# A layer of hybrid mixers and a mixture of experts on one core: the last expert block's second weight and its turned rows in places of their own, overflow branches nested, filler transposes

## What is computed

```python
def s5_mixer(...):            # one of the three mixers
    ...
    z = jax.nn.gelu(y)
    out = z * jax.nn.sigmoid(z @ w_glu)          # "GLU", 1024x256 @ 256x256

def hier_moe(h, w_grp, b_grp, w_exp, b_exp, w1, w3, w2):
    g_sel = argmax(xf @ w_grp + b_grp)           # 1 of 4 groups
    top_p, top_i = top_k(softmax(exp_logits[rows, g_sel]), 2)   # 2 of its 8 experts
    ...
    def expert_block(xb, e):                     # a block: 128 rows of one expert
        hb = silu(xb @ w1[e]) * (xb @ w3[e])     # 1024 -> 512
        return hb @ w2[e]                        # 512 -> 1024
    return segment_sum(y_rows * gate, row_tok)

x = x + concat(mixers) @ w_out
x = x + hier_moe(rms_norm(x), ...)
```

## Time and profile before

| | |
|---|---|
| profiled execution, its own time | 1237.19 us |
| its span (first to last instruction) | 1235.0 us |
| PE busy | 1127.7 us (91%) |
| DVE busy | 972.1 us (79%) |
| ACT busy | 703.3 us (57%) |
| POOL busy | 388.1 us (31%) |
| moved from and to HBM | 252.25 MB read, 26.35 MB written |
| median of 3 runs | 1235.97 us |

### The profile page before, as it was taken

The page is one execution under the profiler, slowest core; times in us unless marked ns, Lnnn a source line. Parts: engine busy times, 40 slices in busy tenths (PEclk is TensorE's granted clock), DMA queues, the critical chain, the costliest instruction groups (busy, mean ns, idle before and its releaser), DMA issues.

```text
span 1235.0 us, 15931 instructions
## 1 busy us (share of the span) xinstructions
PE 1127.7 (91%) x5636; PEld 867.3 (70%) x5636; DVE 972.1 (79%) x1182; ACT 703.3 (57%) x820; POOL 388.1 (31%) x359
## 2 busy tenths in 40 slices
PE   5979999889999799994999999999999999999992
PEld 3437565656676577873788888888877877787781
DVE  1999999656766653377799999999989989898971
ACT  5611224655565541223577777777777777777751
POOL 2330007377971000113022232233343332233221
PEclk8989999899999899995899999999999999999996
DMA  6700010000005012227799999999999999999940
GB/s 196 177 1 1 0 19 10 2 1 1 2 1 239 1 35 85 102 103 279 312 378 369 369 392 385 386 394 396 382 361 380 373 358 371 373 349 367 356 136 10
DMA packets 55484, 260.93 MB, mean 211 GB/s; under 512 B 31088, under 2 KB 31760, under 8 KB 41616
## 3 DMA queue, kind: packets, MB, share of 16 engines
q1 hardware_dynamic: 45344, 243.03, 51.2%
q0 software_dynamic: 10096, 17.34, 5.9%
HBM read 252.25 MB, written 26.35 MB: 226 GB/s over the span
## 4 chain that ended last, share of the span: by engine, by line
PE 65%; DMA 13%; DVE 11%; ACT 4%; issue 4%; SPq 2%; POOL 1%; DVEq 0%; ACTq 0%; POOLq 0%
PE psum L2122 24%; DMA w<-in_w 12%; PE psum L2142 9%; PE psum L2034 7%; PE psum L1952 4%; PE psum L1762 3%; DVE arena L1112 3%; PE psum L1982 3%; PE psum L1800 3%; PE psum L1970 2%; PE psum L2112 2%; PE psum L1840 1%; DVE arena L1115 1%; DVE am L1439 1%; PE psum L1844 1%
## 5 line engine op out<-in xcount | busy, mean ns | idle before, releaser
L1606 DVE TENSOR_TENSOR w_rest<-w,w_high 128x2048 fp32r<-128x2048 f32 x136 | 305.2, 2286 | 19.0 <-ACT w_high L1033 18.5
L1033 ACT ACTIVATE w_high<-w 128x2048 fp32r<-128x2048 f32 x136 | 256.4, 1912 | 76.0 <-DMA w<-in_w 58.2
L2122 PE MATMUL psum<-w_high,xgT_high 128*128 128x512 f32 x544 | 217.7, 400 | 13.8 <-DVE xgT_rest L1652 13.8
L2122 PE MATMUL psum<-w_rest,xgT_high 128*128 128x512 f32 x544 | 213.7, 393 | 0.0
L2122 PE MATMUL psum<-w_high,xgT_rest 128*128 128x512 f32 x544 | 213.1, 392 | 0.0
L1659 DVE TENSOR_TENSOR w_rest<-w,w_high 128x2048 fp32r<-128x2048 f32 x68 | 152.5, 2284 | 2.1 <-ACT w_high L1043 2.1
L1043 ACT ACTIVATE w_high<-w 128x2048 fp32r<-128x2048 f32 x68 | 126.4, 1908 | 24.1 <-DMA w<-in_w 24.1
L2122 PEld LDWEIGHTS psum<-w_high,xgT_high 128*128 128x128 f32 x544 | 102.9, 189 | 39.2 <-issue 16.4
L692 POOL DMA_INDIRECT out<-arena,idx x34 | 94.5, 2780 | 107.3 <-DVE arena L1672 102.0
L2122 PEld LDWEIGHTS psum<-w_rest,xgT_high 128*128 128x128 f32 x544 | 102.8, 189 | 22.1
L2122 PEld LDWEIGHTS psum<-w_high,xgT_rest 128*128 128x128 f32 x544 | 103.1, 190 | 20.3
(11 more groups left out here) (272 smaller groups left out, 2029.8 us busy)
## 6 DMA issues: line engine op xcount, KB each, us to landing
w<-in_w SPq DMA_DIRECT2D x102, 2048.0 KB, 19.0
arena<-in_x SPq DMA_DIRECT2D x5, 1024.0 KB, 4.9
h_scratch<-arena SPq DMA_DIRECT2D x8, 512.0 KB, 2.6
out<-arena SPq DMA_DIRECT2D x8, 512.0 KB, 3.6
arena<-in_x SPq DMA_DIRECT2D x1, 3072.0 KB, 20.3
arena<-in_w_in SPq DMA_DIRECT2D x1, 2688.0 KB, 16.5
arena<-in_w_in SPq DMA_DIRECT2D x1, 2048.0 KB, 12.2
wout_y_raw<-in_w_out SPq DMA_DIRECT2D x1, 2048.0 KB, 9.1
```

What stands on the lines that cost most here:

```text
L1033: act.activation(w13h[k][:, c, :], w13[b][k][:, c, :], ACT.Copy).then_inc(W13H_READY[k], 1)
L1606: dve.tensor_tensor(w13l[b][k][:, c, :], w13[b][k][:, c, :], w13h[k][:, c, :].bitcast(F32), S_).then_inc(W13_SPLIT[k], 1)
L2122: last = pe.matmul(psum[:, k, :], x_[:, c, :], w_[:, c, :], start=(c == 0 and n == 0), stop=(c == KC - 1 and n == 2))
```

## The change

1. **Last block's second weight.** The high part of the last block's `w2` goes into `w1`'s high buffer (`w2h_last`), its turned hidden rows into the buffers of `xgT` (`heTh_last`, `heTl_last`), and its output into PSUM banks 0 and 1. ACT makes the two halves of `w2h_last` right after `high_heT(NS - 2)`, DVE takes the rests around `hidden(NS - 1)`, PE turns the last hidden rows between the two halves of `down(0, NS - 2)`.
2. **Overflow loop.** On all engines the second branch of a pass is nested in the first. On POOL the wait for the last scatter stands behind the loop (and inside it where a block is taken).
3. **Routing.** `picks_ready` and `slots_ready` are raised twice per part, so PE starts each product earlier; `table` runs k outermost.
4. **First gather.** POOL issues it straight from the table, then prepares the indices; DVE waits for `idxs_copied` before it goes on with `rest_w13` of block 0.
5. **Order at blocks 0 and 1.** PE does `turn_rows(1)` before `overflow_table()`, DVE `rest_xgT(1)` before it waits for that table.
6. **Filler transposes.** `keep_busy` writes transposes of `ident` to banks that nobody reads: 16 between the halves of `z`, 28, 28 and 36 in the routing, 14 after `turn_rows(0)`.

```diff
+        w2h_last = w13h[0].rearrange("p c n -> p (c n)").rearrange("p (f d) -> p f d", f=FC)
+        heTh_last, heTl_last = xgTh[:, 0:FC, :], xgTl[:, 0:FC, :]
...
# POOL
-            gather(0, 0)
+            settle()
+            pool.indirect_dma_start(out=xg[0], out_offset=None, in_=h2_d,
+                                    in_offset=bass.IndirectOffsetOnAxis(ap=tabi[:, 0, 0:1], axis=0),
+                                    bounds_check=T - 1, oob_is_err=False).then_inc(ROWS_IN[0], 16)
+            prepare(0, 0)
+            pool.tensor_copy(idx[:, 0, :], tabi[:, 0, :]).then_inc(idxg_copied, 1)
             gather(1, 1)
-            prepare(0, 0)
...
+            with pool.Fori(0, OVF // 2 - 1) as it:
+                with pool.If(n_ov > 2 * it + FIRST_OV):
+                    pool.wait_ge(Y_OUT[1], 8 * NS)
+                    ov_rows(0, it)
+                    with pool.If(n_ov > 2 * it + (FIRST_OV + 1)):
+                        ov_rows(1, it)
             pool.wait_ge(Y_OUT[1], 8 * NS)
-            with pool.Fori(0, OVF // 2 - 1) as it:
-                for b in range(2):
-                    with pool.If(n_ov > 2 * it + (FIRST_OV + b)):
...
# ACT
             high_heT(NS - 2)
+            act.wait_ge(W2_IN[1], 8 * NS)
+            for c in (slice(0, FC // 2), slice(FC // 2, FC)):
+                act.activation(w2h_last[:, c, :], w2s[1][:, c, :], ACT.Copy).then_inc(w2h_ready, 1)
+            act.wait_ge(heT_filled, NS)
+            act.activation(heTh_last.rearrange("p c n -> p (c n)"), psum[:, 2, :], ACT.Copy).then_inc(heTh_saved, 1)
             save_y(0, NS - 2)
-            for h in range(2):
-                high_w2(1, NS - 1, h, W2_IN[1], 8 * NS)
-            high_heT(NS - 1)
-            save_y(1, NS - 1)
...
# DVE
                 tt(both[:, i0:i1], pick[0][:, i0:i1], pick[1][:, i0:i1], A_)
+                dve.sem_inc(picks_ready, 1)
...
-                dve.sem_inc(slots_ready, 1)
+                for k in range(2):
+                    tt(rowhot[:, k, i0:i1, :], iota_j[:, :].unsqueeze(1).to_broadcast([P, n_t, P]),
+                       rw[:, k].unsqueeze(2).to_broadcast([P, n_t, P]), ALU.is_equal)
+                    dve.sem_inc(slots_ready, 1)
...
             dve.sem_inc(y_saved_v, 1)
+            dve.wait_ge(idxs_copied, 1)
             rest_w13(0, 0, 0, (1,))
...
# PE
+            def keep_busy(bank, n):
+
+                for _ in range(n):
+                    pe.transpose(bank[:, 0:P], ident[:, :], ident[:, :])
...
+                if c == 0:
+                    keep_busy(lo(F_Z(1, 1)), 16)
...
             table(0)
+            keep_busy(psum[:, 0, :], 28)
             ranks(1)
+            keep_busy(psum[:, 0, :], 28)
             table(1)
+            keep_busy(psum[:, 0, :], 36)
...
             turn_rows(0, 0, 16)
+            keep_busy(psum[:, 0, :], 14)
...
             up(1, 0, 0)
+            turn_rows(1, 1, 16)
             overflow_table()
-            turn_rows(1, 1, 16)
...
-            down(0, NS - 2)
-            turn_hidden(NS - 1)
-            down(1, NS - 1)
+            down(0, NS - 2, turn_last=True)
+
+            pe.wait_ge(heT_saved, NS)
+            pe.wait_ge(w2_split, 2 * NS)
+            parts = ((heTh_last, w2h_last), (heTl_last, w2h_last), (heTh_last, w2l[1]))
...
```

More of the change, by code:

```diff
@@ L1707, in _ @@
             hidden(0)
+            rest_xgT(1)
             dve.wait_ge(ov_filled, 1)
@@ L1710, in _ @@
             dve.sem_inc(ov_tab_ready, 1)
-            rest_xgT(1)
             rest_w13(1, 1, 1)
@@ L2075, in table @@
                 i0, i1 = ROUTE[part]
-                pe.wait_ge(slots_ready, part + 1)
-                for i in range(i0, i1):
-                    for k in range(2):
+                for k in range(2):
+                    pe.wait_ge(slots_ready, 2 * part + k + 1)
+                    for i in range(i0, i1):
                         last = pe.matmul(psum[:, 1, 0:2 * NE], rowhot[:, k, i, :], blkval[:, k, i].rearrange("p v e -> p (v e)"),
@@ L2129, in turn_hidden, with down @@
                 last.then_inc(heT_filled, 1)
-            def down(b, e):
+            def down(b, e, turn_last=False):
                 pe.wait_ge(heT_saved, e + 1)
@@ L2143, in down @@
                                              start=(c == 0 and n == 0), stop=(c == FC - 1 and n == 2))
+                    if turn_last and k == 0:
+                        turn_hidden(e + 1)
                 last.then_inc(y_filled, 1)
@@ L2169, in _, with ov_products @@
             up(1, 1, NS - 1)
-            down(0, NS - 2)
-            turn_hidden(NS - 1)
-            down(1, NS - 1)
+            down(0, NS - 2, turn_last=True)
+            pe.wait_ge(heT_saved, NS)
+            pe.wait_ge(w2_split, 2 * NS)
+            parts = ((heTh_last, w2h_last), (heTl_last, w2h_last), (heTh_last, w2l[1]))
+            for k in range(2):
+                for c in range(FC):
+                    for n, (h_, w_) in enumerate(parts):
+                        last = pe.matmul(psum[:, k, :], h_[:, c, :], w_[:, c, 512 * k:512 * (k + 1)],
+                                         start=(c == 0 and n == 0), stop=(c == FC - 1 and n == 2))
+            last.then_inc(y_filled, 1)
+            def ov_products(b, it):
+                e = 2 * it + (NS + b)
+                turn_rows(b, e, 16 * it + 16 * (NS // 2 + 1))
+                pe.wait_ge(xgT_saved, e + 1)
+                up(0, b, e)
+                up(1, b, e)
+                turn_hidden(e)
+                down(b, e)
             pe.wait_ge(ov_table, 1)
@@ L2176, in _ @@
             with pe.Fori(0, OVF // 2 - 1) as it:
-                for b in range(2):
-                    with pe.If(n_ov > 2 * it + (FIRST_OV + b)):
-                        e = 2 * it + (NS + b)
-                        turn_rows(b, e, 16 * it + 16 * (NS // 2 + 1))
-                        pe.wait_ge(xgT_saved, e + 1)
-                        up(0, b, e)
-                        up(1, b, e)
-                        turn_hidden(e)
-                        down(b, e)
+                with pe.If(n_ov > 2 * it + FIRST_OV):
+                    ov_products(0, it)
+                    with pe.If(n_ov > 2 * it + (FIRST_OV + 1)):
+                        ov_products(1, it)
 _INS = ["x", "positions", "mix_norm", "w_in", "q_a_norm", "w_uq", "kv_a_norm", "w_ukv", "q_norm", "k_norm",
```

111 lines of the change are left out of this document (66 added, 45 removed).

## The result

The changed kernel takes 1216.66 us, the median of 4 runs (1215.32 to 1220.37), against 1235.91 us for the kernel before on the same chip: a ratio of 0.986 with a 95% interval from 0.9835 to 0.9884, so 17.3 us less (14.3 to 20.4). The two medians by themselves lie 19.2 us apart, which this interval takes in. The forecast was 1219.0 us, its range 1212.5 to 1225.5. The profiled execution took 1220.37 us, the longest of the first four, with a span of 1218.5.

A forecast was written before the change was run, and what follows sets the result against it. The prediction took saturated DMA weight loads to bound the expert loop, with stalls in the chain at the end. Gains of 7.7 + 4.7 + 3.0 + 1.4 = 16.8 us from 1235.97 gave 1219.2, stated as 1219.0, range 1212.5 to 1225.5.

The forecast's parts named there:

- last block: End of the program: the stall before the last `down` goes, so the last scatter is issued at 1212.0 instead of 1219.74, 7.7 us less.
- loop ahead of the wait: POOL's overflow loop runs while the last scatter lands, with the DRAIN keeping its 5.96 us: 4.7 us less.
- GLU fillers: GLU product: 16 transposes in PE's 2.2 us gap keep the clock high, 6.8 instead of 9.88 us, 3.0 us less.
- routing to block 0: From ranks to block 0: first rank product and table leave the path, DVE becomes the bound, 1.4 us less.
- order at blocks 0 and 1: PE some 6 to 8 us ahead at block 1, but loads come no sooner: nothing gained at the end.
- rival 4: Stall before the last `down` partly stays because the last `w2` lands 3 us later than read: 1222 us; chance 0.07.
- the 0.8 us for the first rank product: Routing: only the first rank product, 0.80 us for its two rows, leaves the path; the split one-hot adds some 0.1.
- rival 3: Routing and GLU: fillers run at the low clock, block 0 starts later and the GLU gains 0: 1228 us; chance 0.09.
- The loads do not come sooner: Expert loop: DMA engines are saturated from its start, so PE, ahead at block 1, only meets its waits some blocks earlier.
- Rival 2: Expert loop: PE's lead from block 1 survives to the end, some 6 us more gain: 1213 us; chance 0.12.
- PE's lead at block 1: Start of the expert loop: PE some 6 to 8 us ahead of before, as `overflow_table` covers the copies.

## Why the prediction was right, step by step

| step | forecast, us | measured, us |
|---|---|---|
| last block | -7.7 | -7.75 (last scatter from `down` of block 32) |
| loop ahead of the wait | -4.7 | -4.4 (end from the last scatter) |
| GLU fillers | -3.0 | -2.5 |
| routing to block 0 | -1.4 | -0.2 |
| order at blocks 0 and 1 | 0 | -2 to -4 (medians with and without it) |
| sum | -16.8 | -17 to -19; the whole change -17.3 |

**Last block, right.** `w2` was there in time, so rival 4 has fallen; the product of block 32 ended 5.93 us after its start and the last began at once, 5.5 us long; the last scatter was held by the landing before it. Two links were off and nearly cancel: from the scatter of block 32 to the index copy it was 5.98 us of 5.79 taken, and from that copy to the last issue 0.65 of 0.95.

**Loop, right.** A pass took 0.47 us of 0.45 taken. The DRAIN has the same 5957 ns in all traces, whatever stands ahead of it.

**GLU, right in kind, 0.5 us too large.** The product starts at the high clock and stays there, 7.16 instead of 6.8 us (the prediction's 32 x 0.20 + 0.3 is 6.7). Whether all 2.5 us reach the end is not shown: the attention steps behind it vary. The last logits products end at 553.2 to 558.4 us in the four traces without these fillers, 555.9 in the mean, and at 552.8 to 556.0 in the ten with them, 554.6 in the mean, so 1.3 us earlier, with a scatter larger than that. In the changed kernel the first eight score products took 5.17 us, 0.65 each, at a clock of 0.67 between 248.2 and 253.3; in the kernel with the GLU fillers only four of them took 1.97, 0.49 each. The two runs of the changed kernel differ in such places: its 36 first products with `w_out` took 10.19 us in the one trace and 8.66 in the other.

**Routing, the step that was mis-sized.** The failed term is the 0.8 us for the first rank product, the only one that was to leave the path. From the end of the logits products to the end of the ranks it was 8.6 us before (558.37 to 567.01) and 8.8 in the changed kernel (555.94 to 564.71). Without the fillers it is 8.3, so the split product gives 0.3 us, since its second half waits for the later picks, and the first 28 fillers take 0.45 back. The prediction had their late end in rival 3 alone. DVE's first rest therefore starts 14.6 us after the logits, where it was 14.2. The bound named (DVE, with `rest_xgT(0)` right behind its three rests) was the right one. Its new wait was under-sized: DVE stands 2.56 us (573.13 to 575.69), where the forecast had 2.2, and its three rests start 1.9 us later after the logits than before (19.75 against 17.84 us), where the forecast had 0.6. Taking that wait out does not help by itself: POOL's issue of the gather and its copies then stand beside a working DVE. Timeline of POOL, the changed kernel and then the one without the wait:

```profile
574.25 1.20 POOL L705 DMA_INDIRECT arena<-h_scratch,arena  x1 [18.31 <-issue]
575.46 0.20 POOL L691 COPY idx<-arena 128x2 int32<-128x2 int32 x1
```

```profile
573.83 2.49 POOL L705 DMA_INDIRECT arena<-h_scratch,arena  x1 [18.33 <-issue]
576.32 1.17 POOL L691 COPY idx<-arena 128x2 int32<-128x2 int32 x1
577.44 2.25 POOL L709 COPY idx<-arena 128x2 int32<-128x2 int32 x1
```

The issue doubles, from 1.20 to 2.49 us, and block 0 then waits for the gathered rows and starts only 0.5 us sooner. The Trainium skill, page GPSIMD Engine Reference, section Specifications, says that GpSimd shares its memory interface with VectorE and contends with instructions of two SBUF inputs, which a rest of `w` is; the two timelines agree.

**Order, the step that failed.** "The loads do not come sooner" is wrong. It was read from a DMA share of 1.00 over the whole of 620 to 885 us, which says nothing of the first loads, where what can be loaded depends on how fast PE frees buffers. The new order lets PE finish block 1's first product sooner, and the stream moves 0.5 to 0.8 MB more in those 80 us. So the loop has no single bound: PE's lead counts as far as the stream can use it, and the stream's lead as far as PE frees buffers for it. Rival 2 had the right sign here and too large a size (6 us). PE's lead at block 1 was over-sized too: 6 to 8 us were forecast, and block 1 starts at 600.77 where it started at 605.89, 5.1 us earlier, of which 2.7 lie behind the logits.

**What made the number right** is in part luck, since the misses cancel: 1.2 us too much for routing and 0.5 for GLU and 0.3 for the loop, against 2 to 4 too little for the order.

**Rival 3** has fallen in its time and in the GLU part, but not for the first fillers of the routing. From 558.9 us on PE ran nothing but fillers, at a clock of 0.50 until 563.0, and at 1.00 from 563.2; they end at 564.10, and the rank products follow. The rows of the changed kernel, PE alone:

```profile
558.90:563.00 4.10, 4.10 (x21) 0.50 1.09 334
563.20:564.60 1.40, 1.40 (x16) 1.00 0.67 272
...
571.00:574.90 3.90, 3.90 (x36) 1.00 1.07 447
```

A filler takes 0.20 us in the first row (4.10 / 21) and 0.11 in the last. At 0.11 each the 28 would have ended at 562.0, ahead of the sum at 563.10: that they were late is the low clock of their first 21. The later ones did run at the high clock, and it bought no time, since PE was not what block 0 waited for.

The Trainium skill, page TensorE: Matmul & The Clock Gate, section PE-mode transpose, says that transpose mode does not engage the full clock. The clock rose here while PE ran fillers alone, which speaks against that rule for these instructions. The trace lists a filler as a plain MATMUL, though, and an ordinary product of the same shape takes as long (two of L2120 in 0.22 us), so whether a filler runs in that mode is not shown. The prediction's own evidence was weaker: it read the rise from durations at the program's start, and the earlier trace rows give a clock of 1.00 for both of those stretches.

## What to carry to other kernels

A saturated queue of loads with a single reload slot per buffer is a loop of two engines: before writing off a lead of one, look at the stretch in which the queue fills, not at the one in which it is full, and try both leads together. Work that follows a last transfer belongs ahead of the wait for it; and of a stall at the end, count everything behind it, since each engine's last steps have their own floor (here the landing of the scatter before). Fillers for the clock pay where the next product on the chain is PE's own (2.5 us for 16 in the GLU part); where another engine is late they bought nothing and delayed what was queued behind them. Block 0 did run faster where they reached almost up to it (10.9 to 11.3 us instead of 12.8), but no run tests that by itself.

The best of the kernels run are those with the wait of DVE taken out and block 1's `w2` loaded early: 1214.49 and 1214.21 us, 4 us below the changed kernel. Both edits on the kernel with the GLU fillers only were not tried.

## What was not expected of the hardware

- The DRAIN that closes POOL's stream takes 5957 ns in every trace here, 4.8 us after the landing of the last scatter or right behind it. No run shows what it waits for.
- A run of narrow products was followed by a low clock. In the changed kernel PE was busy for all of the stretch from 597.3 to 600.7 us with the overflow table (32 products of 32 columns), at a clock of 1.00, and the 24 wide products right behind it took 7.30 us at a mean of 0.77:

```profile
597.30:600.70 3.40, 3.40 (x31) 1.00 1.00 424
600.80:608.00 7.20, 7.20 (x25) 0.77 1.00 425
```

  It is no accident of one execution. The 24 products behind the table take 7.2 to 7.3 us in all five traces with the new order and the DVE wait, and 5.72 and 5.75 us in two of the three without that wait (8.25 in the third). Where the old order lets PE idle ahead of block 1 they take 7.3 to 8.5. What decides it is open.
- An indirect DMA's issue and a copy of 256 numbers on POOL take twice to eleven times as long beside a subtraction on DVE: 1.20 and 0.20 us against 2.49 and up to 2.25.
